# First norm from row sums, and a new order of the opening 80 microseconds, in a two-layer streaming encoder on one core

## The chip, the cores and the metric
One core of a Trainium2 chip runs the whole program. The metric is the device time of one execution in microseconds (us), the median of several runs. Five engines work side by side and meet at semaphores: TensorE (PE in the profile, its weight loads are PEld), VectorE (DVE), ScalarE (ACT), GpSimd (POOL) and SyncE (SP), which here only issues transfers. ScalarE issues transfers as well; SPq and ACTq are the rows of their queues.

## The reference
The input x is 512 frames of 1024 channels in float32, with one conditioning vector c. Each of two layers does the following; `ada` gives shift, scale and gate vectors from c.

```python
c_act = silu(c)
for l in range(DEPTH):                                   # DEPTH = 2
    ada = (c_act @ w_ada[l] + b_ada[l]).reshape(B, 9, 1024)
    u = modulate(rmsnorm(x, norm_g[l, 0]), ada[:, 0], ada[:, 1])   # xn * (1 + scale) + shift
    x = x + 0.5 * ada[:, 2] * swiglu(u, w_ff1_up[l], w_ff1_down[l])  # 1024 -> 2 x 2816 -> 1024
    u = modulate(rmsnorm(x, norm_g[l, 1]), ada[:, 3], ada[:, 4])
    x = x + ada[:, 5] * token_mixing(u, ..., sinks[l], cos, sin)   # windowed attention with rope, pooling, gates
    u = modulate(rmsnorm(x, norm_g[l, 2]), ada[:, 6], ada[:, 7])
    x = x + 0.5 * ada[:, 8] * swiglu(u, w_ff2_up[l], w_ff2_down[l])
```

cos and sin come from the integer positions and are first used in token mixing, as are the sinks (one logit a head).

## The kernel before
The activations lie transposed: a tile `x_t` holds 128 channels on the partitions and 512 frames along the free dimension, eight such pieces k = 0 to 7. A matrix product is a row of *tiles*: tile n gives 128 output channels for all 512 frames in one of five PSUM banks. Every product is made of float32 numbers split in a high and a low part, so that a tile has three matmuls a piece k: high weights by `u_hi`, high weights by `u_lo`, low weights by `u_hi`, 24 in all for 1024 input channels. ScalarE makes the high part of a weight tile, `w_hi` (L639, in the opening L781 in `first_weights`), and counts `hi_ready`; GpSimd makes the low part `w_lo` (L588) in place of the loaded weights and counts `lo_ready`. Weights arrive two tiles to a load in three slots `stage` (L491), ordered by SP: a slot is loaded again when TensorE has finished the tile that used it last.

The first half layer (`ff_half(0, 0, 0)`) has 22 up tiles (gate and value in turn) and 8 down tiles. For each pair ScalarE makes `silu` (L678), VectorE the product, `h_hi` and `h_lo` (L1003, L1006, L1008). Between these VectorE adds up 24 pieces of `w_ada` for the later vectors (`ada_piece`, L973 and L977, from the tile 3 of the half on), each loaded by SP in the same queue as the weights and each waiting until VectorE has used an older one.

The opening is written by hand, because the first norm and the first modulation vectors (`ada[:, 0]` and `ada[:, 1]`) are not there yet:
- `turn_x(j)` (L1601) transposes 128 frames of x_rows into two banks; VectorE copies one (L1263) and ScalarE the other (L761) to `x_t`. ScalarE squares `x_t` (L768), VectorE adds the squares over the eight pieces (`sum_squares`, L1222), and TensorE adds them over the partitions with a column of ones (L1671).
- Two calls of 12 small VectorE steps each (`rsqrt_step`, L826 to L837, two columns a call) give the reciprocal root, and TensorE spreads it over the partitions into ps6 (L1677).
- The modulation vectors come in four blocks b of 256 channels. For each block TensorE multiplies c_act by 2 MB of `ada_block` (`block_sums`, L1615, 64 small matmuls), VectorE copies the rows (L1231), TensorE turns them (`block_turn`, L1624), and VectorE makes shift and scale (L1236, L1238) and `xs` for the two pieces k of the block (L1249). ScalarE rounds them to `u_hi` (L789), VectorE makes `u_lo` (L1253).
- `block_tiles(b)` (L1638 to L1653) multiplies the two pieces of block b into four tiles at once (banks 0 to 3), so that tiles 0 to 3 are all done when block 3 is. TensorE's order is: sums, turn and tiles of block 0; sums and turn of 1; then sums and turn of b + 1 before the tiles of b; last the tiles of 3. Then tile 4 begins the ordinary order.
- Before tile 4 can start, `ff_half` of ScalarE first waits for tile 0 to make its silu and only then makes the high part of tile 4; the low part of tile 4 is GpSimd's. In block 0 VectorE makes the low parts of tiles 0 to 2, GpSimd that of tile 3.
- ScalarE's queue issues the small loads: c, constants and row vectors at the start; positions (L769, 256 KB broadcast) and sinks (L774, four loads of 256 single floats each) behind its last square. VectorE makes the rope angle in eight steps (`angle_step`) behind blocks 1 and 2, ScalarE its sine and half-angle sine in block 2 (L796, L797), VectorE finishes both behind block 3 (L1280 to L1284).
- SP issues, in order: x in four loads, block 0, stage slots 0 and 1, blocks 1 and 2, slot 2 (tiles 4 and 5), block 3. Its first `ada_piece` waits for all four block sums.

Of the kernel before, what the change touches and what calls it, by code (L numbers as in the profile page):

```python
# [160 lines left out]
def trunk(nc, x, c, positions, w_ada, b_ada, norm_g, w_ff1_up, w_ff1_down, w_in, q_norm_g, k_norm_g,  # L161
          sinks, w_pool_grp, pool_scale, w_attn_o, w_pool_o, w_out, w_ff2_up, w_ff2_down, consts, out):
    ctx = ExitStack()
    with ctx:
# [40 lines left out]
        x_sq = [at(f"x_sq{i}", [P, KT, P], F32, o) for i, o in enumerate((r_h + 5 * KT * BLOCK_W * 4, r_a))]  # L205
# [35 lines left out]
        pos_i = at("pos_i", [P, S], I32, r_g + KB2)  # L241
        angle = at("angle", [P, S], F32, r_g + 2 * KB2)
        turns = at("turns", [P, S], F32, r_g + 3 * KB2)
# [107 lines left out]
        x_summed = sem("x_summed")  # L351
# [54 lines left out]
        def newton_before(call):  # L406
            return call * NEWTON
# [52 lines left out]
        def _(sp):  # L460
# [99 lines left out]
            ada_block_load(2)  # L560
            up_load(first_up, 0, 0, 2)
            ada_block_load(3)
# [20 lines left out]
        def _(pool):  # L583
# [27 lines left out]
            pool.wait_ge(lo_ready, AHEAD)  # L611
            for l in range(DEPTH):
                for half in range(2):
                    for n in range(FF_TILES):
                        low_part("ff", tiles_before(l, 0, half), n + AHEAD)
# [17 lines left out]
        def _(act):  # L633
# [34 lines left out]
            def ff_half(l, i, half):  # L668
                tiles, loads = tiles_before(l, i, half), loads_before(l, i, half)
                for n in range(FF_TILES):  # L670
                    if START_TILES <= tiles + n + AHEAD < DEPTH * TILES:
                        round_weights("ff", tiles, loads, n + AHEAD)
                    if n < 2 * HALF_FT and n % 2 == 0:
                        j = n // 2
                        act.wait_ge(tile_done, tiles + n + DONE)
                        if j >= 2:
                            act.wait_ge(product_ready, products_before(l, i, half) + j - 1)
                        nc.scalar.activation(silu[:, j % 2, :], bank[n % BANKS][:, :], ACT.Silu  # L678
                                             ).then_inc(silu_ready, 1)
                    if n >= 2 * HALF_FT and half == 1 and event(l, i) + 1 < 3 * DEPTH:  # L680
                        square_tile(event(l, i) + 1, n - 2 * HALF_FT)

# [59 lines left out]

            act.dma_start(c_rows[:, :], c.rearrange("b (r c) -> (b r) c", c=P)).then_inc(c_in, 16)
            act.dma_start(consts_s[:, :], consts).then_inc(c_in, 16)
# [14 lines left out]
            for j in range(JT):  # L759
                act.wait_ge(turned, 2 * j + 2)  # L760
                nc.scalar.activation(x_t[:, 4:KT, j * P:(j + 1) * P],  # L761
                                     bank[(2 * j + 1) % 4][:, :].rearrange("p (m f) -> p m f", f=P), ACT.Copy
                                     ).then_inc(x_kept_act, 1)
                act.wait_ge(x_kept, j + 1)
                act.wait_ge(x_kept_act, j + 1)
                if j >= 2:
                    act.wait_ge(x_summed, j - 1)
                nc.scalar.activation(x_sq[j % 2][:, :, :], x_t[:, :, j * P:(j + 1) * P], ACT.Square).then_inc(x_squared, 1)  # L768
            act.dma_start(pos_i[:, :], positions[0].partition_broadcast(P)).then_inc(late_in, 16)  # L769
            with nc.allow_non_contiguous_dma(reason="eight sinks"):  # L770
                for i in range(DEPTH):
                    for t in range(2):

                        act.dma_start(sink_all[t * CHUNK:(t + 1) * CHUNK, i, :],  # L774
                                      sinks[i].rearrange("(b t) -> t b", t=2)[t].partition_broadcast(CHUNK)
                                      ).then_inc(late_in, 16)
# [6 lines left out]
            for b in range(BLOCKS):  # L783
# [10 lines left out]
                if b == 2:  # L794
                    act.wait_ge(setup_step, DEPTH + 8)
                    nc.scalar.activation(sin_t[:, :], angle[:, :], ACT.Sin).then_inc(act_step, 1)  # L796
                    nc.scalar.activation(cos_t[:, :], angle[:, :], ACT.Sin, scale=0.5).then_inc(act_step, 1)  # L797
# [20 lines left out]
        def _(dve):  # L818
# [52 lines left out]
            def stats_step(l, i, h, step):  # L871

                if step == 0:
                    dve.wait_ge(norm_summed, 2 * event(l, i) + (h + 1 if l or i else 2))
# [118 lines left out]
            def ff_half(l, i, half):  # L993
                tiles = tiles_before(l, i, half)
                count = products_before(l, i, half)
                for n in range(FF_TILES):
# [22 lines left out]
                    if n == 18 and half == 0:  # L1019
                        make_gate(l, i, half)  # L1020
                    if 0 <= n - ADA_STEP < ff_pieces(l, i, half):
# [197 lines left out]
            def sum_squares(j):  # L1219

                dve.wait_ge(x_squared, j + 1)
                nc.vector.tensor_reduce(sq_sum[:, j * P:(j + 1) * P], x_sq[j % 2][:, :, :].rearrange("p m f -> p f m"), AX_X,  # L1222
                                        ALU.add).then_inc(x_summed, 1)

# [16 lines left out]
            def block_u(b):  # L1241

                dve.wait_ge(first_vec, 2 * b + 2)
                for k in (2 * b, 2 * b + 1):
                    if k == 0:
                        dve.wait_ge(rstd_spread, 2)
                    if k >= 4:
# [7 lines left out]

            for l in range(DEPTH):
# [4 lines left out]
            for j in range(JT):  # L1261
                dve.wait_ge(turned, 2 * j + 1)
                nc.vector.tensor_copy(x_t[:, 0:4, j * P:(j + 1) * P],  # L1263
                                      bank[2 * j % 4][:, :].rearrange("p (m f) -> p m f", f=P)).then_inc(x_kept, 1)
                if j:
                    sum_squares(j - 1)
            sum_squares(JT - 1)
            for h in range(2):
                stats(0, 0, h)
            for b in range(BLOCKS):  # L1270
                block_vectors(b)
                block_u(b)
                if b == 0:
                    for n in range(AHEAD):
                        low_part("ff", 0, n)
                if b in (1, 2):
                    for step in range(4 * (b - 1), 4 * b):
                        angle_step(step)
            dve.wait_ge(act_step, 3)
            nc.vector.tensor_scalar(sin_t[:, :], sin_t[:, :], consts_s[:, K_SIGN:K_SIGN + 1], None, ALU.mult  # L1280
                                    ).then_inc(setup_step, 1)
            nc.vector.tensor_tensor(cos_t[:, :], cos_t[:, :], cos_t[:, :], ALU.mult).then_inc(setup_step, 1)
            dve.wait_ge(setup_step, DEPTH + 10)
            nc.vector.tensor_scalar(cos_t[:, :], cos_t[:, :], -2.0, 1.0, ALU.mult, ALU.add).then_inc(setup_step, 1)  # L1284
# [31 lines left out]
        def _(pe):  # L1316
# [276 lines left out]
            def turn_x(j):  # L1593

                pe.wait_ge(x_in[j], 16)
                for h in range(2):
                    g = 2 * j + h
                    if g >= 4:
                        pe.wait_ge((x_kept, x_kept_act)[h], j - 1)
# [26 lines left out]
            def block_tiles(b):  # L1626


                pairs = (2 * b, 2 * b + 1)
                for k in pairs:  # L1630
                    pe.wait_ge(u_hi_ready, 2 * k + 2)
                    if b == 0:
                        pe.wait_ge(u_lo_ready, 2 * k + 2)
                    for n in range(START_TILES):
                        hi, lo = hi_tile(n, KT), stage_tile(w_lo, "ff", n)
                        if b == 0 and k == 0:
                            pe.wait_ge(hi_ready, n + 1)
                        mm(bank[n][:, :], hi[:, k, :], u_hi[:, k, :], start=(k == 0), stop=False)  # L1638
                        if b == 0:
                            mm(bank[n][:, :], hi[:, k, :], u_lo[:, k, :], start=False, stop=False)  # L1640
                        else:
                            mm(bank[n][:, :], lo[:, k, :], u_hi[:, k, :], start=False, stop=False)
                    if b:
                        pe.wait_ge(u_lo_ready, 2 * k + 2)
                        for n in range(START_TILES):
                            last = mm(bank[n][:, :], hi_tile(n, KT)[:, k, :], u_lo[:, k, :], start=False, stop=(k == KT - 1))
                            if k == KT - 1:
                                last.then_inc(tile_done, 1)
# [90 lines left out]
```

## Time and profile before

| what | us |
|---|---|
| median of 3 runs (lowest to highest) | 2077.24 (2074.61 to 2077.28) |
| profiled execution, its own time | 2076.52 |
| its span, first to last instruction | 2074.7 |
| TensorE busy | 2038.8 |
| VectorE, GpSimd, ScalarE busy | 953.7, 673.8, 553.7 |
| chain that ended last: TensorE, VectorE, transfers | 95%, 3%, 1% |
| mean granted TensorE clock | 0.997 |

The profile lists, for each instruction, when it started and how long it ran, and for an idle engine what ended its idle time. The span of the profiled execution is 1.8 us shorter than its own time; the rest lies around the program.

### The profile page before, as it was taken

The numbers are of one execution on the slowest core, as the hardware profiler recorded it, in microseconds if no ns is written. First come the engines' busy times: TensorE is split into PE (matmuls) and PEld (weight loads), VectorE is DVE, ScalarE is ACT, GpSimd is POOL, SyncE is SP. The second block draws the span as 40 slices with busy tenths as digits, with TensorE's granted clock in tenths as the row PEclk, the third lists the DMA queues.
The fourth block names the chain that finished last, engine by engine and source line by source line (L and its number), as shares of the span: only waits on it lengthen the run. The fifth ranks groups of instructions, "written<-read, shape, count | busy, mean of one in ns | idle before, by whom it ended". The sixth has DMA issues, their size and how long they took to land.

```text
span 2074.7 us, 24433 instructions
## 1 busy us (share of the span) xinstructions
PE 2038.8 (98%) x10117; PEld 1700.4 (82%) x10117; DVE 953.7 (46%) x1389; ACT 553.7 (27%) x808; POOL 673.8 (32%) x274
## 2 busy tenths in 40 slices
PE   5999999999999999999999999999999999999999
PEld 4788888897888987888898888889878888888888
DVE  5654255366546755211256533445555666221121
ACT  2222122233422422122232211223243233221220
POOL 0345435502000245443434542452100004543451
PEclk9999999999999999999999999999999999999999
DMA  9465366522224366333326654652221435332331
GB/s 274 132 203 183 112 182 199 132 72 69 73 68 130 91 204 188 118 98 109 126 70 177 203 157 125 200 184 66 72 82 61 120 124 142 100 104 82 101 106 67
DMA packets 329066, 264.78 MB, mean 128 GB/s; under 512 B 24878, under 2 KB 310910, under 8 KB 328958
## 3 DMA queue, kind: packets, MB, share of 16 engines
q1 hardware_dynamic: 327296, 262.70, 42.6%
q8 instruction: 80, 1.31, 0.3%
q10 hardware_dynamic: 1662, 0.54, 0.1%
q14 instruction: 28, 0.23, 0.0%
HBM read 261.11 MB, written 2.10 MB: 127 GB/s over the span
## 4 chain that ended last, share of the span: by engine, by line
PE 95%; DVE 3%; DMA 1%; issue 1%; ACT 0%; POOL 0%; ACTq 0%; DVEq 0%
PE bank L1328 27%; PE bank L1330 27%; PE bank L1329 27%; PE bank L1404 1%; PE bank L1408 1%; PE bank L1405 1%; PE bank L1355 1%; PE bank L1357 1%; PE bank L1356 1%; PE ps L1537 1%; PE ps L1519 1%; DMA stage<-in_w_out 1%; PE ps L1495 0%; PE bank L1638 0%; PE ps L1502 0%
## 5 line engine op out<-in xcount | busy, mean ns | idle before, releaser
L588 POOL TENSOR_TENSOR w_lo<-stage,w_hi 128x1024 fp32r<-128x1024 f32 (+1 forms) x237 | 647.3, 2751 | 1210.3 <-ACT w_hi L639 1171.1
L1328 PE MATMUL bank<-u_hi,w_hi 128*128 128x512 f32 x1768 | 698.7, 395 | 3.7 <-POOL w_lo L588 3.5
L1330 PE MATMUL bank<-u_hi,w_lo 128*128 128x512 f32 x1768 | 689.3, 390 | 0.0
L1329 PE MATMUL bank<-u_lo,w_hi 128*128 128x512 f32 x1768 | 688.7, 390 | 0.0
L639 ACT ACTIVATE w_hi<-stage 128x1024 fp32r<-128x1024 f32 (+2 forms) x336 | 349.5, 1074 | 585.6 <-DMA stage<-in_w_ff_up 334.5
L1328 PEld LDWEIGHTS bank<-u_hi,w_hi 128*128 128x128 f32 x1768 | 332.4, 188 | 78.7 <-issue 10.8
L1329 PEld LDWEIGHTS bank<-u_lo,w_hi 128*128 128x128 f32 x1768 | 332.5, 188 | 69.6 <-issue 2.4
L1330 PEld LDWEIGHTS bank<-u_hi,w_lo 128*128 128x128 f32 x1768 | 332.2, 188 | 70.0
L1003 DVE TENSOR_TENSOR prod<-silu,bank 128x512 f32<-128x512 f32 x88 | 60.5, 688 | 522.3 <-PE bank L1330 503.9
L1328 PE MATMUL bank<-h_hi,w_hi 128*128 128x512 f32 x744 | 290.2, 390 | 1.0 <-DVE h_lo L1008 1.0
L1330 PE MATMUL bank<-h_hi,w_lo 128*128 128x512 f32 x744 | 289.5, 389 | 0.0
L1329 PE MATMUL bank<-h_lo,w_hi 128*128 128x512 f32 x744 | 289.5, 389 | 0.0
L919 DVE SCALAR_TENSOR_TENSOR x_t<-bank,gate,x_t 128x512 f32<-128x512 f32 (+1 forms) x92 | 62.6, 680 | 332.5 <-PE bank L1330 301.7
L977 DVE SCALAR_TENSOR_TENSOR ada_acc<-ada_stage,c_act,ada_acc 128x1024 f32<-128x1024 f32 x112 | 205.3, 1833 | 5.4 <-DVE ada_acc L977 0.9
L1328 PEld LDWEIGHTS bank<-h_hi,w_hi 128*128 128x128 f32 x744 | 139.6, 188 | 31.4 <-DVE h_lo L1008 1.5
L1330 PEld LDWEIGHTS bank<-h_hi,w_lo 128*128 128x128 f32 x744 | 139.7, 188 | 29.0
L1329 PEld LDWEIGHTS bank<-h_lo,w_hi 128*128 128x128 f32 x744 | 139.7, 188 | 28.8
L678 ACT ACTIVATE silu<-bank 128x512 f32<-128x512 f32 x88 | 52.5, 596 | 404.2 <-PE bank L1330 389.9
L843 DVE TENSOR_TENSOR w_lo<-stage,w_hi 128x1024 fp32r<-128x1024 f32 (+1 forms) x103 | 108.5, 1057 | 101.6 <-ACT w_hi L639 101.3
L1008 DVE TENSOR_TENSOR h_lo<-prod,h_hi 128x512 fp32r<-128x512 f32 x88 | 112.6, 1280 | 3.0
L1006 DVE CAST h_hi<-prod 128x512 fp32r<-128x512 f32 x88 | 72.8, 827 | 3.0
L650 ACT ACTIVATE squares<-x_t 128x512 f32<-128x512 f32 (+1 forms) x45 | 24.2, 538 | 155.9 <-DVE sq_sum L938 122.7
(176 smaller groups left out, 1488.2 us busy)
## 6 DMA issues: line engine op xcount, KB each, us to landing
stage<-in_w_ff_up SPq DMA_DIRECT2D x176, 512.0 KB
ada_stage<-in_w_ada SPq DMA_DIRECT2D x128, 512.0 KB, 4.8
stage<-in_w_ff_down SPq DMA_DIRECT2D x32, 1408.0 KB
stage<-in_w_in SPq DMA_DIRECT2D x18, 1024.0 KB
ada_block<-in_w_ada SPq DMA_DIRECT2D x8, 1024.0 KB, 12.1
stage<-in_w_out SPq DMA_DIRECT2D x8, 1024.0 KB
stage<-in_w_in SPq DMA_DIRECT2D x16, 256.0 KB
stage<-in_w_in SPq DMA_DIRECT2D x8, 512.0 KB
```

The costliest lines, as they stand in the source:

```text
L588: nc.gpsimd.tensor_tensor(stage_tile(w_lo, kind, n), t, hi_tile(n, depth(kind, n)), ALU.subtract).then_inc(lo_ready, 1)
L639: nc.scalar.activation(hi_tile(n, depth(kind, n)), stage_tile(stage, kind, n), ACT.Copy).then_inc(hi_ready, 1)
L678: nc.scalar.activation(silu[:, j % 2, :], bank[n % BANKS][:, :], ACT.Silu).then_inc(silu_ready, 1)
L843: nc.vector.tensor_tensor(stage_tile(w_lo, kind, n), stage_tile(stage, kind, n), hi_tile(n, depth(kind, n)), ALU.subtract).then_inc(lo_rea ...
L919: nc.vector.scalar_tensor_tensor(x_t[:, m, frames], product[:, frames], gate[:, i, m:m + 1], x_t[:, m, frames], ALU.mult, ALU.add).then_in ...
L977: nc.vector.scalar_tensor_tensor(ada_acc[:, :], ada_stage[a % ADA_SLOTS][:, :], c_k, ada_acc[:, :], ALU.mult, ALU.add).then_inc(ada_used, 1)
L1003: nc.vector.tensor_tensor(prod[:, j % 2, :], silu[:, j % 2, :], bank[n % BANKS][:, :], ALU.mult).then_inc(product_ready, 1)
L1006: nc.vector.tensor_copy(h_hi[:, j, :], prod[:, j % 2, :]).then_inc(h_hi_ready, 1)
L1008: nc.vector.tensor_tensor(h_lo[:, j, :], prod[:, j % 2, :], h_hi[:, j, :], ALU.subtract).then_inc(h_lo_ready, 1)
L1328: mm(bank[n % BANKS][:, :], hi[:, k, :], rhs_hi(k), start=(k == 0), stop=False)
L1329: mm(bank[n % BANKS][:, :], hi[:, k, :], rhs_lo(k), start=False, stop=False)
L1330: last = mm(bank[n % BANKS][:, :], lo[:, k, :], rhs_hi(k), start=False, stop=(k == k_n - 1))
```

## The change
The squares are taken by ScalarE from `x_rows`, where a frame's 1024 channels lie along the free dimension, with the accumulator giving the sum of each frame (`x_ss`, 128 x 4). One call of 12 steps works on all four columns. `sum_squares`, the products with the column of ones, and the second call are gone. TensorE turns all four parts of x in a row; VectorE copies six of the eight banks, ScalarE two. Constants are loaded ahead of c. VectorE makes the low parts of tiles 0 to 3; GpSimd starts with tile 4. ScalarE makes the high part of tile 4 in block 2, between the `u_hi` of blocks 2 and 3. Block 3 is loaded before slot 2. `block_tiles` is put in another order: tiles 0 and 1 first in block 0, starting when the first `u_hi` is there; from block 1 on the next block's sums lie between its two pieces k, and the next block's turn inside the second. Positions and sinks are loaded by ScalarE at tile 2 of the first half, the eight angle steps lie at tiles 6 to 13 of VectorE's half, the sines at tile 15 of ScalarE's, the last three steps at tile 17 of VectorE's.

```diff
-        x_sq = [at(f"x_sq{i}", [P, KT, P], F32, o) for i, o in enumerate((r_h + 5 * KT * BLOCK_W * 4, r_a))]
+        x_sq = [at(f"x_sq{i}", [P, D], F32, o) for i, o in enumerate((r_h + 5 * KT * BLOCK_W * 4, r_a))]
...
+            ada_block_load(3)
             up_load(first_up, 0, 0, 2)
-            ada_block_load(3)
...
-            pool.wait_ge(lo_ready, AHEAD)
+            pool.wait_ge(lo_ready, START_TILES)
...
-                    for n in range(FF_TILES):
+                    for n in range(0 if l or half else START_TILES - AHEAD, FF_TILES):
                         low_part("ff", tiles_before(l, 0, half), n + AHEAD)
...
# ScalarE, ff_half
-                    if START_TILES <= tiles + n + AHEAD < DEPTH * TILES:
+                    if START_TILES < tiles + n + AHEAD < DEPTH * TILES:
                         round_weights("ff", tiles, loads, n + AHEAD)
...
+                    if l + i + half == 0 and n == 2:
+                        positions_load()
+                    if l + i + half == 0 and n == 15:
+                        act.wait_ge(setup_step, DEPTH + 8)
+                        nc.scalar.activation(sin_t[:, :], angle[:, :], ACT.Sin).then_inc(act_step, 1)
+                        nc.scalar.activation(cos_t[:, :], angle[:, :], ACT.Sin, scale=0.5).then_inc(act_step, 1)
...
+            def positions_load():
+                act.wait_ge(u_lo_ready, U_STEPS)
+                act.dma_start(pos_i[:, :], positions[0].partition_broadcast(P)).then_inc(late_in, 16)
... (the four loads of the sinks, as before)
# ScalarE, opening
+            act.dma_start(consts_s[:, :], consts).then_inc(c_in, 16)
             act.dma_start(c_rows[:, :], c.rearrange("b (r c) -> (b r) c", c=P)).then_inc(c_in, 16)
-            act.dma_start(consts_s[:, :], consts).then_inc(c_in, 16)
...
             for j in range(JT):
+                act.wait_ge(x_in[j], 16)
+                if j >= 2:
+                    act.wait_ge(x_squared, j - 1)
+                nc.scalar.activation(x_sq[j % 2][:, :], x_rows[:, j, :], ACT.Square, accum_out=x_ss[:, j:j + 1]
+                                     ).then_inc(x_squared, 1)
+            for j in (2, 3):
                 act.wait_ge(turned, 2 * j + 2)
                 nc.scalar.activation(x_t[:, 4:KT, j * P:(j + 1) * P],
                                      bank[(2 * j + 1) % 4][:, :].rearrange("p (m f) -> p m f", f=P), ACT.Copy
                                      ).then_inc(x_kept_act, 1)
-                act.wait_ge(x_kept, j + 1)
-                act.wait_ge(x_kept_act, j + 1)
-                if j >= 2:
-                    act.wait_ge(x_summed, j - 1)
-                nc.scalar.activation(x_sq[j % 2][:, :, :], x_t[:, :, j * P:(j + 1) * P], ACT.Square).then_inc(x_squared, 1)
...
                 if b == 2:
+                    first_weights(START_TILES)
...
# VectorE, ff_half
+                    if l + i + half == 0 and 6 <= n < 14:
+                        angle_step(n - 6)
+                    if l + i + half == 0 and n == 17:
+                        angles_done()
...
# VectorE, opening
+            for g in (0, 1, 2, 3, 4, 6):
+                j, h = divmod(g, 2)
+                dve.wait_ge(turned, g + 1)
+                nc.vector.tensor_copy(x_t[:, 4 * h:4 * h + 4, j * P:(j + 1) * P],
+                                      bank[g % 4][:, :].rearrange("p (m f) -> p m f", f=P)).then_inc(x_kept, 1)
+            dve.wait_ge(x_squared, JT)
+            for step in range(NEWTON):
+                rsqrt_step(0, x_ss[:, :], slice(0, JT), D, step)
...
-                    for n in range(AHEAD):
+                    for n in range(START_TILES):
                         low_part("ff", 0, n)
...
# TensorE, block_tiles
+                if b == 0:
+                    for n0 in range(0, START_TILES, 2):
+                        for k in range(2):
+                            for part, ready in ((u_hi, u_hi_ready), (u_lo, u_lo_ready)):
+                                if n0 == 0:
+                                    pe.wait_ge(ready, 2 * k + 2)
+                                for n in (n0, n0 + 1):
+                                    if k == 0 and part is u_hi:
+                                        pe.wait_ge(hi_ready, n + 1)
+                                    mm(bank[n][:, :], hi_tile(n, KT)[:, k, :], part[:, k, :], start=(k == 0 and part is u_hi),
+                                       stop=False)
+                        for n in (n0, n0 + 1):
+                            pe.wait_ge(lo_ready, n + 1)
+                            for k in range(2):
+                                mm(bank[n][:, :], stage_tile(w_lo, "ff", n)[:, k, :], u_hi[:, k, :], start=False, stop=False)
+                    return
+                for k in (2 * b, 2 * b + 1):
                     pe.wait_ge(u_hi_ready, 2 * k + 2)
                     for n in range(START_TILES):
+                        mm(bank[n][:, :], hi_tile(n, KT)[:, k, :], u_hi[:, k, :], start=False, stop=False)
+                        mm(bank[n][:, :], stage_tile(w_lo, "ff", n)[:, k, :], u_hi[:, k, :], start=False, stop=False)
+                    if k % 2 and b + 1 < BLOCKS:
+                        block_turn(b + 1)
+                    pe.wait_ge(u_lo_ready, 2 * k + 2)
                     for n in range(START_TILES):
+                        last = mm(bank[n][:, :], hi_tile(n, KT)[:, k, :], u_lo[:, k, :], start=False, stop=(k == KT - 1))
+                        if k == KT - 1:
+                            last.then_inc(tile_done, 1)
+                    if k % 2 == 0 and b + 1 < BLOCKS:
+                        block_sums(b + 1)
```

## Rows read from the trace of the kernel before

**Rows 1.** The page: span, busy line, tenths of 40 slices for TensorE and its clock
```profile
span 2074.7 us, 24433 instructions
PE 2038.8 (98%) x10117; PEld 1700.4 (82%) x10117; DVE 953.7 (46%) x1389; ACT 553.7 (27%) x808; POOL 673.8 (32%) x274
...
PE   5999999999999999999999999999999999999999
```
**Rows 2.** Waits of TensorE from 76.2 us on: total us, times, longest
```profile
PE bank L1328 <- POOL w_lo L588: 3.5, 1, 3.5
PE ps L1373 <- DVE sq_sum L938: 1.6, 2, 1.0
```
**Rows 3.** Timeline 0 to 40 us: start, length, engine, instruction, idle time before
```profile
6.83 0.27 PE L1657 MATMUL ps<-consts_s,c_rows 8*128 8x8 f32 x1 [6.83 <-DMA consts_s<-in_consts]
...
7.03 3.67 PE L1601 MATMUL bank<-consts_s,x_rows 128*128 128x128 f32 x16
...
12.39 1.06 ACT L768 ACTIVATE x_sq<-x_t 128x1024 f32<-128x1024 f32 x1 [2.76 <-DVE x_t L1263]
...
15.35 0.69 DVE L1263 COPY x_t<-bank 128x512 f32<-128x512 f32 x1
...
18.37 3.68 DVE L1222 TENSOR_REDUCE sq_sum<-x_sq 128x128 f32<-128x1024 f32 x2
...
23.15 0.16 DVE L826 TENSOR_SCALAR nw_v<-ps 128x2 f32<-128x2 f32 x1 [1.11 <-PE ps L1671]
...
25.39 0.15 DVE L826 TENSOR_SCALAR nw_v<-ps 128x2 f32<-128x2 f32 x1
...
25.62 1.19 PE L1677 MATMUL ps<-consts_s,nw_y 128*128 128x128 f32 x4 [2.51 <-DVE nw_v L826]
...
28.93 3.53 PE L1615 MATMUL ps<-ada_block,c_act 128*32 128x128 f32 x64
...
34.56 1.38 ACT L789 ACTIVATE u_hi<-xs,shift_b 128x512 fp32r<-128x512 f32 x2 [10.83 <-DVE xs L1249]
...
35.38 1.42 DVE L1253 SCALAR_TENSOR_TENSOR u_lo<-xs,shift_b,u_hi 128x512 fp32r<-128x512 f32 x2 [0.26 <-ACT u_hi L789]
...
36.23 0.77 PE L1638 MATMUL bank<-u_hi,w_hi 128*128 128x512 f32 x1 [3.02 <-ACT u_hi L789]
...
36.71 3.49 DVE L843 TENSOR_TENSOR w_lo<-stage,w_hi 128x1024 fp32r<-128x1024 f32 x3
```
**Rows 4.** By line and form, ScalarE: count, busy us, mean ns, idle before
```profile
L693 ACT ACTIVATION_READ_ACCUMULATOR probs<-ps,neg_max 128x1 f32 x64 | 13.0, 203 | 0.0
```
**Rows 5.** Timeline 43 to 77 us, blocks 1 to 3 and tile 4
```profile
43.39 1.95 PE L1615 MATMUL bank<-ada_block,c_act 128*32 128x128 f32 x64
...
45.76 0.33 PE L1624 MATMUL ps<-consts_s,block_rows 128*128 128x128 f32 x1 [0.41 <-DVE block_rows L1231]
...
47.43 1.38 ACT L789 ACTIVATE u_hi<-xs,shift_b 128x512 fp32r<-128x512 f32 x2 [9.60 <-DVE xs L1249]
...
71.60 1.07 PE L1646 MATMUL bank<-u_lo,w_hi 128*128 128x512 f32 x4
72.03 0.60 ACT L678 ACTIVATE silu<-bank 128x512 f32<-128x512 f32 x1 [7.55 <-PE bank L1646]
...
73.65 5.14 POOL L588 TENSOR_TENSOR w_lo<-stage,w_hi 128x1024 fp32r<-128x1024 f32 x2 [30.97 <-ACT w_hi L639]
...
76.15 0.47 PE L1328 MATMUL bank<-u_hi,w_hi 128*128 128x512 f32 x1 [3.48 <-POOL w_lo L588]
```
**Rows 6.** Windows: length, busy by engine (count), granted TensorE clock, DMA share, GB/s
```profile
48.00:51.70 3.70, 0.00 (x0) 0.00 (x0) 3.29 (x7) 0.81 (x2) 0.00 (x0) 1.00 0.67 208
...
52.60:56.00 3.40, 3.40 (x10) 2.62 (x9) 3.14 (x5) 1.39 (x2) 0.00 (x0) 0.51 0.00 0
76.20:79.90 3.70, 3.70 (x10) 2.91 (x11) 3.50 (x4) 1.94 (x2) 3.39 (x2) 0.55 0.30 72
79.90:85.00 5.10, 5.10 (x24) 4.24 (x23) 5.00 (x3) 0.67 (x2) 4.40 (x2) 0.99 0.00 0
```
**Rows 7.** Windows of the transfers, same columns
```profile
24.00:33.00 9.00, 5.99 (x73) 4.95 (x73) 3.39 (x21) 0.00 (x0) 0.00 (x0) 1.00 0.47 120
34.00:50.00 16.00, 11.32 (x153) 8.83 (x153) 9.71 (x15) 4.66 (x6) 2.40 (x1) 0.89 1.10 338
...
51.00:61.00 10.00, 9.29 (x89) 7.31 (x89) 6.18 (x12) 2.54 (x4) 0.00 (x0) 0.83 0.01 3
```
**Rows 8.** Queues from 24 to 33 us: packets, MB, share; the sinks' issue and landing
```profile
q1 hardware_dynamic: 1071, 1.08, 40.9%
q10 hardware_dynamic: 978, 0.00, 5.7%
...
L774 ACTq DMA_DIRECT2D sink_all<-in_sinks x4: 637/656/753, 18.9 to 21.0; - x4
...
DMA to landing us min/median/max: 7.0/9.8/13.4
```
**Rows 9.** Timeline of SP, ScalarE, GpSimd, VectorE: the load for tiles 8 and 9
```profile
85.27 1.08 SPq L491 DMA_DIRECT2D stage<-in_w_ff_up  x2
...
92.33 2.01 ACT L639 ACTIVATE w_hi<-stage 128x1024 fp32r<-128x1024 f32 x2 [8.25 <-DMA stage<-in_w_ff_up]
...
93.47 4.76 POOL L588 TENSOR_TENSOR w_lo<-stage,w_hi 128x1024 fp32r<-128x1024 f32 x2 [9.17 <-ACT w_hi L639]
...
99.86 0.69 DVE L1003 TENSOR_TENSOR prod<-silu,bank 128x512 f32<-128x512 f32 x1 [6.42 <-PE bank L1330]
```

## Prediction on record
> **What bounds the kernel.** I read the page first. TensorE is busy 2038.8 of 2074.7 us, and only the first of the 40 slices shows it half idle [rows 1]. Then the waits of TensorE from tile 4 on: the largest is the 3.5 us in front of tile 4 itself, the next 1.6 us in two pieces [rows 2]. So behind the opening the time is a fixed train of matmuls, and whatever the opening gives, the end gives, unless a new wait appears in the first half. The question is when tile 4 starts and whether the train stays whole after it. Before, it starts at 76.15 us [rows 5]. Right behind its wait, from 76.2 to 79.9, the granted clock is 0.55, that is mostly at the lower level of 1.2 GHz; from 79.9 on it is 0.99 [rows 6]. 24 matmuls take 5.46 us on the fast clock (5.10 us hold 22.4 of them at 0.2275 us each); 3.7 us at 0.55 lose 1.7 us. Tile 4's start is thus worth 77.85 us on the fast clock.
>
> **The path before**, on the timeline [rows 3]: constants land at 6.83, transposes of half of x, then VectorE's reductions of squares (two of them 3.68 us, the last ends at 22.05), sums over partitions, two calls of 12 small steps (the first from 23.15, the second from 25.39), spreading, and the first block sums at 28.93. TensorE's first product starts at 36.23.
>
> **The first norm.** The constants are issued first instead of second: worth 0 to 0.65 us (the issue of c takes 0.6), I take 0.4. TensorE starts at 6.4, and 33 transposes at 3.67/16 = 0.23 us run to 14.0, if the copies keep pace: 0.69 us for a bank on VectorE against 0.92 us for its four transposes, so they do. The bank that VectorE copies last is turned at 13.1 and copied at 13.8. ScalarE's squares are 1.06 us each [rows 3]; reading the accumulator adds 0.20, as it does behind the exponentials [rows 4]. Four of them from 6.9 end at 12.0, ahead of that copy, so they lie beside it. The 12 steps took 25.39 - 23.15 = 2.24 us plus a tail of 0.1 with two columns; two or four columns make no difference I can see, since fixed cost is nearly all of it. They end at 16.1; the copies of the row vectors add 0.5, the spreading of four columns 1.2 (the row has 1.19). Block sums 0 start at 17.8 instead of 28.93: **11.1 us earlier**. Block 0's transfer is not in the way: it is second in SP's queue, and at some 300 GB/s its 2 MB behind 2.4 MB lie in place at 15.
>
> **Block 0.** The same steps follow with the same lengths, so the first `u_hi` (35.24 before) is there at 24.1 and TensorE starts there, without the wait for `u_lo`. ScalarE must have made the high parts of tiles 0 and 1 by then; they need slot 0, which lands by 21.7 at the latest (before, ScalarE took it up then, straight behind its issues). VectorE's `u_lo` ends at 25.7 (36.80 - 11.1). Its four low parts at 3.49/3 = 1.16 us end at 30.3; the fourth was GpSimd's. TensorE needs one more tile's low matmuls behind that: 30.8 at the earliest. With all 24 matmuls on the slow clock (0.43 us) it would be 34.5. I take 31.8, slow for the first eight as before. It was 43.4: **11.6 us earlier**.
>
> **Blocks 1 to 3** (29.0 us before, from 43.46 to 72.45). Work: 72 matmuls at 0.228 are 16.4 us, three sums at 1.95 are 5.85, turns 1.0. The new waits: sums to turned rows and back, 0.35; from the end of the turn (46.10) to the first `u_hi` (48.12) 2.02 us [rows 5], bare in block 1. In blocks 2 and 3 only the four `u_lo` matmuls (0.91 us) cover it, which leaves 1.1 us each. Sum 27.9 us, so **the last tile of block 3 ends at 59.8**. The order of before has no bare wait in blocks 2 and 3, but it lost 3.7 us bare at 48 to 51.7 and 1.7 us of clock behind it (0.51 in 52.6 to 56) [rows 6]. Whether the 2.0 us wait in block 1 also costs the clock no row decides: the idle 48 to 51.7 and 72.7 to 76.15 did, gaps of 0.4 did not. 0 or 1.7 us; I take 0, nearer in shape to neither, since a turn lies in its middle.
>
> **Transfers.** From 34 to 50 us they run at 338 GB/s, from 24 to 33 at 120, and after 51 at 3: all of the opening's 14 MB lies there at 51 [rows 7]. In the slow stretch the sinks' queue moves 978 packets and no bytes to speak of, and the weight queue is down to 41% [rows 8]. I read the dip as the sinks'; 9 us at 120 in place of 338 are 5.8 us. Without it the last transfer ends at 45, and counting back 1 MB (3.2 us) for slot 2 and 2 MB (6.2 us) for each block, block 3 is there at 42, block 2 at 35.6, block 1 at 29.4. Needed: block 1 at 31.8, block 2 at 39.3, block 3 at 48.2, slot 2 at 47.5. All hold. With the dip as it was, block 1 at 35.2 costs 3.4 us, the others little.
>
> **Tile 4.** Its high part is made at 47.5, GpSimd's low part (2.4 us) is done by 51. Nothing stands before it at 59.8, and the clock stays up. What covered nothing before (silu 0, `w_hi`, `w_lo`, 3.7 us) now falls to tile 5, behind tile 4's 5.46 us: `w_hi` 1.04 and GpSimd 2.4 to 2.85 end some 4 us after tile 3.
>
> **Moved into the first half.** ScalarE's issues take 3.2 us behind the silu of tile 2; the next load, for tiles 6 and 7, lands at about the same time and is needed 5 us later. VectorE's 11 angle steps of 0.4 to 0.7 us lie in gaps of 2 to 6 us between products. The sinks' dip now falls on the load for tiles 8 and 9. Before, it was issued at 85.27, its high part made at 92.33, its low part done at 95.85, and tile 8 began at 99.8 [rows 9]: 3.9 us to spare. If the dip moves as it is, it lies 7 to 16 us after tile 4's start, this load is issued at 9, and 1.5 MB (with an `ada` piece) lose up to 4 us: a stall of 0 to 1, up to 3 if the piece ahead suffers too. I take 0.5. The Trainium skill, "DMA: Bandwidth & Descriptors", says in "Rules for kernel authors" that a non-contiguous last dimension is lowered to one descriptor an element, and in "Queues, rings and completion order" that each engine takes turns between queues packet by packet; the 978 packets agree. By that rule the cost goes along with the load wherever it stands, which speaks against this part of the change; it would give the second rival below.
>
> **Sum.** 77.85 - 59.8 = 18.05, less 0.5, is 17.5 us. Span 2074.7 - 17.5 = 2057.2; 1.8 us lie around it, and the profiled execution (2076.52) is 0.7 under the median: 2059.7 us.
>
> **Rivals.**
> (1) The start-up has more bare waits than I count: a clock loss of 1.7 us in block 1, 1 to 2.7 us in block 0, or the blocks' data late by 3.4. Price 3 to 6 us: about 2064. For it: four hand-overs between VectorE, ScalarE and TensorE are now bare. Against: each is priced above from a row. 0.15.
> (2) The sinks' packets stall the train at tile 8 (or 6) by 2 to 4 us, with up to 1.7 us of clock: about 2063. For it: the margin of 3.9 us equals the loss. Against: the queues are emptier there, and before, the dip needed 5 us to set in. 0.15.
> (3) Nothing gained: slot 2, now last, holds up ScalarE, which waits for it in its own order ahead of the `u_hi` of block 3. This decides from a landing at 53 on, and 15 us are lost only from 68 on; the rows have everything at 51. 0.03.
> (4) Slower: VectorE's first angle step waits for the sinks, and behind it in VectorE's order stand the `ada` pieces, behind these in SP's order the weights. VectorE gets there some 14 us after tile 4's start; the loads have 4 us to spare; to lose 22 us the sinks would have to land 40 us after it, that is 35 us after their issue. The row's worst is 13.4. 0.03.
>
> **Numbers.** The forecast's own case has 0.64: 2056 to 2062. With (1) and (2) the range is 2056 to 2067. 0.2% is 4.2 us, about what a measurement of this kernel can tell from no change. Faster by more 0.94, within it 0.03, slower 0.03.
>
> **What the next profile would show.** Block sums 0 at about 17.8; first product at 24; no TENSOR_REDUCE before it; tile 4 at 59.8 without a wait and with the clock at 1.00; the dip of the transfers at 67 to 76 in place of 24 to 33, with q10's packets; TensorE's waits from tile 4 on as before or with one for `w_lo` at tile 8. Wrong would be: block sums behind a transfer, ScalarE waiting for slot 2 in block 2, VectorE waiting for the positions.

## The result, and the profile after

The changed kernel takes 2061.73 us (median of 4 runs, 2060.99 to 2064.09) against 2077.26 before: ratio 0.9926, 95% interval 0.9914 to 0.9939, so 15.5 us faster. The forecast was 2059.7, with 2056 to 2067 around it. The profiled execution has a span of 2059.9 us, 14.8 less than [rows 1].

The opening of the changed kernel on the timeline (start, length, engine, instruction, idle time before), to be laid beside [rows 3, 5]:

```profile
5.25 0.27 PE L1670 MATMUL ps<-consts_s,c_rows 8*128 8x8 f32 x1 [5.25 <-DMA c_rows<-in_c]
5.45 6.33 PE L1609 MATMUL bank<-consts_s,x_rows 128*128 128x128 f32 x32
...
11.33 0.19 ACT L780 ACTIVATION_READ_ACCUMULATOR x_sq<-x_rows 128x1 f32 x1
11.39 0.69 DVE L1268 COPY x_t<-bank 128x512 f32<-128x512 f32 x1 [0.68 <-PE bank L1609]
...
12.00 0.16 DVE L835 TENSOR_SCALAR nw_v<-x_ss 128x4 f32<-128x4 f32 x1
...
14.78 2.05 PE L1682 MATMUL ps<-consts_s,nw_y 128*128 128x128 f32 x8 [2.81 <-DVE vec L1275]
16.76 2.38 PE L1623 MATMUL ps<-ada_block,c_act 128*32 128x128 f32 x64
...
22.02 0.73 PE L1646 MATMUL bank<-u_hi,w_hi 128*128 128x512 f32 x2 [2.12 <-ACT u_hi L799]
...
28.21 1.07 PE L1651 MATMUL bank<-u_hi,w_lo 128*128 128x512 f32 x4
30.05 1.96 PE L1623 MATMUL bank<-ada_block,c_act 128*32 128x128 f32 x64 [0.78 <-DMA ada_block<-in_w_ada]
...
34.87 0.79 PE L1656 MATMUL bank<-u_hi,w_hi 128*128 128x512 f32 x1 [2.12 <-ACT u_hi L799]
...
45.55 0.50 PE L1656 MATMUL bank<-u_hi,w_hi 128*128 128x512 f32 x1 [1.18 <-ACT u_hi L799]
...
55.13 0.50 PE L1656 MATMUL bank<-u_hi,w_hi 128*128 128x512 f32 x1 [1.58 <-ACT u_hi L799]
...
60.69 0.39 PE L1336 MATMUL bank<-u_hi,w_hi 128*128 128x512 f32 x1
```

The reader sees: VectorE's small steps at 12.0 instead of 23.15, block sums 0 at 16.76 instead of 28.93, and tile 4 (L1336) at 60.7 without a wait, where it had been 76.15 with one of 3.5.

But a wait of the same size stands further on. The waits of TensorE from 59 us on (total, times, longest), beside [rows 2], and the first matmul of tile 8:

```profile
PE bank L1336 <- POOL w_lo L588: 3.5, 1, 3.5
PE ps L1381 <- DVE sq_sum L947: 0.6, 1, 0.6
```
```profile
86.41 0.77 PE L1336 MATMUL bank<-u_hi,w_hi 128*128 128x512 f32 x1 [3.52 <-POOL w_lo L588]
```

Windows of the changed kernel (length, busy by engine, granted clock, DMA share, GB/s), beside [rows 6, 7]:

```profile
35.00:38.40 3.40, 3.40 (x9) 2.68 (x10) 1.33 (x2) 0.47 (x1) 0.00 (x0) 0.53 1.10 348
...
66.50:74.50 8.00, 8.00 (x36) 6.31 (x35) 4.85 (x6) 2.49 (x3) 4.75 (x2) 1.00 0.11 15
...
87.00:90.50 3.50, 3.50 (x12) 2.81 (x11) 3.50 (x3) 1.81 (x2) 2.44 (x2) 0.66 0.26 99
```

From block 1 on, two stretches at mostly 1.2 GHz are left: one behind the bare wait of block 1, one behind the wait at tile 8. (A third lies in front of them: from 14.8 to 16.8 us, under the spreading, the granted clock is 0.50.) And the slow stretch of the transfers is no longer in the opening (348 GB/s there) but at 66.5 to 74.5 us, at 15 GB/s instead of the 120 of [rows 7]. The queues in it (packets, MB, share of 16 engines), and SP's issues:

```profile
q1 hardware_dynamic: 235, 0.11, 5.5%
q10 hardware_dynamic: 910, 0.00, 5.3%
```
```profile
67.48 0.34 SPq L510 DMA_DIRECT2D ada_stage<-in_w_ada  x1
67.87 4.94 SPq L491 DMA_DIRECT2D stage<-in_w_ff_up  x2
```

910 of the sinks' packets pass, and from 68 to 74 us not one packet of the weight queue does. The issue of the load for tiles 8 and 9 alone takes 4.94 us where it took 1.08 [rows 9], and its data come behind the sinks. The `ada` piece ahead of it was issued in the usual 0.34 us and stands still as well: it lands at 77.9 us.

### The profile page after: what moved, and what is told of

The parts are those of the page before. It is cut to its first block, busy times and chain, and to the rows that moved or that the text cites. A ratio compares the mean times of both kernels' runs of the same rounds, so it can differ in the third digit from the quotient of the medians.

```text
span 2059.9 us, 24401 instructions
## 1 busy us (share of the span) xinstructions
PE 2033.6 (99%) x10109; PEld 1695.8 (82%) x10109; DVE 955.3 (46%) x1376; ACT 551.8 (27%) x810; POOL 675.2 (33%) x273
## 4 chain that ended last, share of the span: by engine, by line
PE 95%; DMA 2%; DVE 1%; SPq 1%; ACT 0%; issue 0%; POOL 0%; DVEq 0%; ACTq 0%
PE bank L1336 27%; PE bank L1338 27%; PE bank L1337 27%; PE bank L1412 1%; PE bank L1413 1%; PE bank L1416 1%; PE bank L1363 1%; PE bank L1364 1%; PE bank L1365 1%; DMA stage<-in_w_ff_up 1%; PE ps L1545 1%; PE ps L1527 1%; SPq L491 1%; DMA ada_block<-in_w_ada 1%; PE ps L1434 0%; PE ps L1503 0%
## 5 line engine op out<-in xcount | busy, mean ns | idle before, releaser
L1336 PE MATMUL bank<-u_hi,w_hi 128*128 128x512 f32 x1768 | 698.9, 395 | 3.8 <-POOL w_lo L588 3.5
L1336 PEld LDWEIGHTS bank<-u_hi,w_hi 128*128 128x128 f32 x1768 | 332.5, 188 | 78.7 <-issue 7.3
L1336 PE MATMUL bank<-h_hi,w_hi 128*128 128x512 f32 x744 | 290.1, 390 | 0.0
L1336 PEld LDWEIGHTS bank<-h_hi,w_hi 128*128 128x128 f32 x744 | 139.7, 188 | 30.1 <-issue 1.2
```

The lines of the kernel that those rows point to most:

```text
L1336: mm(bank[n % BANKS][:, :], hi[:, k, :], rhs_hi(k), start=(k == 0), stop=False)
```

## The experiments

**The sinks in one load.** Every partition gets all 16 floats in one piece, and VectorE takes its heads from them when it negates them.

```diff
-                with nc.allow_non_contiguous_dma(reason="eight sinks"):
-                    for i in range(DEPTH):
-                        for t in range(2):
-                            act.dma_start(sink_all[t * CHUNK:(t + 1) * CHUNK, i, :], ...).then_inc(late_in, 16)
+                act.dma_start(sink_raw[:, :], sinks.rearrange("l h -> (l h)").partition_broadcast(P)).then_inc(late_in, 16)
...
-                        nc.vector.tensor_scalar(neg_sink[:, :], sink_all[:, l, :], -1.0, None, ALU.mult).then_inc(sink_ready, 1)
+                        raw = sink_raw[:, :].rearrange("p (l b t) -> p l t b", l=DEPTH, t=2)
+                        for t in range(2):
+                            r = slice(t * CHUNK, (t + 1) * CHUNK)
+                            ins = nc.vector.tensor_scalar(neg_sink[r, :], raw[r, l, t, :], -1.0, None, ALU.mult)
+                        ins.then_inc(sink_ready, 1)
```

> Of the changed kernel, with the four loads of 256 single floats for the sinks replaced by one load of all 16 floats to every partition (128 pieces of 64 bytes), at the same place. Theory: the wait of 3.5 us at tile 8 and the 1.6 us of clock behind it come from the sinks' packets, which hold the weight queue at nearly 0 GB/s from 66.5 to 74.5 us. Then the wait is gone and the time is 2061.7 - 5.1 = 2056.6 us. Rival A: the load for tiles 8 and 9 is late because it stands behind an ada piece in SP's queue: wait stays, 2061.7. Rival B: the 256 KB of the positions are the cause: wait stays, 2061.7.

Measured: 2056.0 us (2054.67 to 2057.45), ratio to before 0.9899 (0.9885 to 0.9914). The wait at tile 8 is gone. The queues of this kernel in the same stretch, 66.5 to 74.5 us, and SP's issue of the same load:

```profile
q1 hardware_dynamic: 2526, 1.88, 85.4%
q10 hardware_dynamic: 29, 0.00, 0.2%
```
```profile
67.99 1.08 SPq L491 DMA_DIRECT2D stage<-in_w_ff_up  x2
```

ScalarE's high part of tile 8 on the timeline, first in the changed kernel, then in this one:

```profile
82.78 2.00 ACT L639 ACTIVATE w_hi<-stage 128x1024 fp32r<-128x1024 f32 x2 [12.24 <-DMA stage<-in_w_ff_up]
```
```profile
75.02 2.01 ACT L639 ACTIVATE w_hi<-stage 128x1024 fp32r<-128x1024 f32 x2 [4.49 <-DMA stage<-in_w_ff_up]
```

The load was issued at the same time (67.87, 67.99) behind the same ada piece, and landed 7.8 us earlier. Rival A falls, and so does B: the positions are still loaded at the same place.

**The same in the kernel before.**

> The kernel before, with the sinks in one load. Theory: the slow stretch of the transfers at 24 to 33 us (120 GB/s) goes to 300 or more, and all of the opening's transfers end at 45 instead of 51 us; the time stays at 2077 within 1 us, since nothing in the opening of this kernel waited for a transfer. Rival: the slow stretch has another cause and stays.

Measured: 2077.53 us, ratio 1.0001 (0.9992 to 1.001). The window of 24 to 33 us, beside the first line of [rows 7], and one in which the transfers of the kernel before had still been running:

```profile
24.00:33.00 9.00, 5.68 (x73) 4.58 (x73) 3.59 (x22) 0.00 (x0) 0.00 (x0) 0.62 1.10 355
...
45.00:51.00 6.00, 2.77 (x88) 2.12 (x77) 4.48 (x10) 1.38 (x2) 0.00 (x0) 1.00 0.04 11
```

355 GB/s instead of 120, all but 0.07 MB moved by 45, and no time gained: the dip was real, and it was hidden. The same load that costs nothing in one kernel costs 5 us in the other.

**The sinks back in the opening**, positions left in the half.

```diff
             for j in (2, 3):
                 ... (ScalarE's two copies of x)
+            with nc.allow_non_contiguous_dma(reason="eight sinks"):
+                ... (the four loads, taken out of positions_load)
```

> Of the changed kernel, with the sinks' four loads back in the opening, behind ScalarE's two copies, and the positions left at tile 2. Theory: the slow stretch of the transfers moves with the sinks to some 18 to 27 us, the second block of w_ada lands at 35 instead of 30 us, TensorE waits for it 6 us instead of 0.8, and the wait at tile 8 (3.5 + 1.6 of clock) goes: the two cancel, 2061 to 2063. Rival B (the positions' 256 KB make the wait at tile 8): both waits, 2067.

Measured: 2062.25 us (2060.82 to 2065.72; the profiled execution is the 2065.72), ratio 0.9929 (0.9912 to 0.9945). The sum was right and its place wrong. No wait for w_lo is left at tile 8, with the positions where they were. But the transfers it slows are not only block 1's: TensorE's waits in this kernel from 15 us on hold

```profile
PE bank L1646 <- ACT u_hi L799: 4.6, 1, 4.6
...
PE bank L1646 <- ACT w_hi L791: 2.6, 2, 2.5
```

against 2.1 and none in the changed kernel. ScalarE waits for slot 0 ahead of the first u_hi, and for slot 1 ahead of tile 2. The rate of all transfers from 19 to 28 us, in 40 equal slices, shows how hard the sinks' packets (the last load lands at 25.9) press here:

```profile
GB/s 19 21 16 7 21 5 3 5 3 5 3 3 0 0 0 0 0 0 0 0 0 1 7 19 110 148 230 273 305 337 346 344 350 346 405 282 280 296 296 305
```

**The high part of tile 4 late again**, in the changed kernel and in the one with one load of the sinks.

```diff
-                    if START_TILES < tiles + n + AHEAD < DEPTH * TILES:
+                    if START_TILES <= tiles + n + AHEAD < DEPTH * TILES:
                         round_weights("ff", tiles, loads, n + AHEAD)
...
-                if b == 2:
-                    first_weights(START_TILES)
```

> Of the changed kernel, with the high part of tile 4 made where it was before the change, behind the silu of tile 0. Tile 4 gets back its wait of 3.5 us and 1.7 us of slow clock. But the load for tiles 8 and 9 is ordered at the same time, so tile 8 then has 5.2 us more to come: its wait of 3.5 us and the slow clock behind it should go. Theory: nothing lost in sum, 2061.7 to 2062.5. Rival: the two waits are independent, 2061.7 + 5.2 = 2066.9.

> As late_w4, with the sinks in one load. No wait at tile 8 is there to be relieved, so the late high part of tile 4 costs its full 3.5 + 1.7 us against one_load: 2056.6 + 5.2 = 2061.8. Rival: it costs nothing here either (then the early high part is worth nothing, 2056.6).

Measured: 2060.54 us (2058.66 to 2061.49) and 2062.4 us (2058.76 to 2062.49). Beside the slow sinks, taking this part of the change back costs nothing (the changed kernel had 2061.73); beside the quick ones it costs 6.4 us against 2056.0, where 5.2 were expected. (One of the four runs beside the quick sinks took 2058.76, so the 6.4 is loose.) In the first, tile 4 waits 3.5 us and tile 8 no more. So in the change as it was made the early high part bought 3.5 us of waiting at tile 4 and paid it back four tiles later. The expectation gave one reason for this, that tile 8 is reached later; the traces show two. The load for tiles 8 and 9 is issued at almost the same time (67.59 against 67.87), but it also lands 2.9 us earlier (ScalarE takes it up at 79.92, in the changed kernel at 82.78); the sinks were issued 1.5 us earlier there.

**The first norm alone**, in the kernel before: squares from x_rows, one call of steps, the transposes in a row, the copies as in the change.

> The kernel before, with the first norm of the changed one alone (squares from x_rows with the accumulator, one call of 12 steps, all of x turned in a row, the same copies). Block sums 0 start 11 to 12 us earlier. Theory: behind that the blocks of w_ada bind, since the sinks' loads still stand in the opening: block 1 lands at about 35, block 2 at 41, so most of the lead is lost in waits for them, 4 to 6 us faster than before, 2072. Rival: the lead stays whole, 2065.

Measured: 2067.29 us (2065.38 to 2069.26), ratio 0.9955 (0.9941 to 0.997), 9.2 us faster: between theory and rival, and outside both. The profile shows the mechanism and a different share (waits of TensorE from 15 us on, three of them):

```profile
PE bank L1634 <- ACT w_hi L782: 5.1, 1, 5.1
...
PE bank L1634 <- DVE u_lo L1250: 3.0, 1, 3.0
...
PE ps L1611 <- DMA ada_block<-in_w_ada: 2.3, 1, 2.3
```

The 3.0 us stood there before the change too (3.02 in [rows 3]). 5.1 us go to slot 1, 2.3 to block 2, both behind the sinks' packets; block 1 is there when it is asked for, since the wait for slot 1 lies ahead of it. I had counted the blocks and left out slot 1, which is ahead of them in SP's queue. SP had issued all of slots 0 and 1 by 17.0 us, before the sinks' packets set in at 19 us, and yet the rate fell far below the 120 GB/s of [rows 7] (again 19 to 28 us in 40 slices):

```profile
5.16 11.86 SPq L491 DMA_DIRECT2D stage<-in_w_ff_up  x4
```
```profile
GB/s 289 262 260 186 66 50 53 64 98 119 85 50 46 55 44 48 37 41 32 46 30 32 14 23 9 9 3 5 5 5 9 12 14 62 146 305 346 353 344 355
```

This run and before_one_load also settle the constants: with c issued first TensorE starts at 6.68 and 6.72, as in [rows 3] (6.83); in the ten traces with the constants first it starts between 5.04 and 5.25.

**The old order of blocks 1 to 3.**

```diff
-                    if k % 2 and b + 1 < BLOCKS:
-                        block_turn(b + 1)
...
-                    if k % 2 == 0 and b + 1 < BLOCKS:
-                        block_sums(b + 1)
...
-            for b in range(1, BLOCKS):
+            for b in range(1, BLOCKS - 1):
+                block_sums(b + 1)
+                block_turn(b + 1)
                 block_tiles(b)
+            block_tiles(BLOCKS - 1)
```

> Of the changed kernel, with TensorE's old order for blocks 1 to 3 (sums and turn of block b + 1 ahead of the tiles of b). Block sums 2 then come at 32 us and wait for their block until 36; tiles 1 start at 38.4 in place of 34.9, but no wait for u_hi is left in blocks 2 and 3 (2.8 us in the changed kernel). Theory: the end of block 3 moves by -1 to +2 us, and the wait at tile 8 moves with it: 2061 to 2064. Rival: the new order is worth its 2.8 us of waits or more, 2059.

Measured: 2061.85 us (2060.99 to 2064.04), no difference from 2061.73 that these runs can tell. The waits change places: no wait for u_hi in blocks 2 and 3, but one of 3.3 us for the transfer of block 2:

```profile
PE ps L1623 <- DMA ada_block<-in_w_ada: 3.3, 1, 3.3
```

The new order of the blocks brings nothing measurable here; the theory holds, the rival falls.

**An earlier turn**, on top of the one load of the sinks.

```diff
                         mm(bank[n][:, :], stage_tile(w_lo, "ff", n)[:, k, :], u_hi[:, k, :], start=False, stop=False)
-                    if k % 2 and b + 1 < BLOCKS:
-                        block_turn(b + 1)
+                        if n == 1 and k % 2 and b + 1 < BLOCKS:
+                            block_turn(b + 1)
```

> As one_load, and in blocks 1 and 2 TensorE turns the next block's rows behind the second of the four tiles instead of behind the fourth. The rows are ready 1.8 us before they are turned, and the waits for the first u_hi of blocks 2 and 3 are 1.2 and 1.6 us: with 0.9 us more of cover they shrink to 0.3 and 0.7, so 1.8 us faster than one_load, about 2054.8. Rival: VectorE or ScalarE is late for another reason there (a gap of 0.5 us before xs in block 3 has no releaser): then 1 us or less.

Measured: 2054.49 us (2053.73 to 2054.68), ratio 0.9891 (0.9877 to 0.9906). The two waits, 1.18 and 1.58 us in the changed kernel, shrink to 0.26 and 0.65 (timeline of this kernel):

```profile
44.65 0.50 PE L1654 MATMUL bank<-u_hi,w_hi 128*128 128x512 f32 x1 [0.26 <-ACT u_hi L793]
...
53.28 0.50 PE L1654 MATMUL bank<-u_hi,w_hi 128*128 128x512 f32 x1 [0.65 <-ACT u_hi L793]
```

**The three once more, in the same rounds on one chip.**

> The changed kernel once more, on the same chip and in the same rounds as the next two, since the intervals of one_load and of the changed kernel touch: 2061.7, with the wait for w_lo at tile 8 in its trace.

> Sinks in one load, repeated beside the changed kernel: 4.5 to 6 us faster than it. If the difference is under 2 us, the wait at tile 8 was a matter of one profiled execution.

> Sinks in one load and the early turn, repeated: 1.5 to 2 us faster than one_load_again, 6.5 to 7.5 faster than changed_again.

Measured: 2062.36 (2060.57 to 2062.97), 2057.52 (2057.0 to 2058.87) and 2054.64 us (2053.56 to 2054.95); the ranges do not touch. One load of the sinks is worth 4.8 us (5.7 in the first runs, which were not taken side by side), the early turn 2.9 more (1.5 in its first rounds). The 2.9 lies above the 1.5 to 2 expected; the trace of one_load_again has 2.0 us of waits for h_lo far behind the opening that the trace of early_turn_again has not, so not all of it need be the turn. The wait at tile 8 is 2.7 us in this execution of the changed kernel. The last kernel, at 0.9895 of before (0.9881 to 0.9908), beats both kernels of the case: 21.6 us faster than before.

## Why the prediction held, and where it did not

**The path bound by TensorE.** Right. What the opening gave, the end gave: tile 4 starts 15.5 us earlier.

**The constants.** Under-priced: 0.4 us taken, 0 to 0.65 as bounds, 1.4 to 1.8 measured (6.68 to 6.83 against 5.04 to 5.25). I had bounded it by the length of the issue in front; the landing moved by more, and no run shows why.

**The first norm.** 11.1 us forecast, 28.93 - 16.76 = 12.2 measured. The transposes run closer together (6.33 us for 32, I had 7.3), the accumulator costs 0.19 as the exponentials' did, squares lie beside the copies. One term was wrong: the spreading takes 2.05 us, not 1.2. The row I used counted one of the two old calls (4 matmuls); there is one call now and it has the matmuls of both (8). They run at a granted clock of 0.50 here; where the clock was 1.00 (late_w4) the same 8 took 1.13 us, so the 1.2 would have been right only on the fast clock.

**Block 0.** Ends at 29.3 against 31.8, since block sums 0 took 2.38 us instead of the 3.53 I had carried over and TensorE starts on the first u_hi at 22.0. The clock of this stretch differs from execution to execution: the spreading and sums take 2.05 and 2.38 us here, 1.13 and 1.95 in late_w4, 1.13 and 3.42 in early_turn.

**Blocks 1 to 3.** 27.9 us forecast, 60.7 - 30.05 = 30.6 measured. 1.6 of the difference are the clock behind the bare wait in block 1 (0.53 over 3.4 us), which I had left at 0 between bounds of 0 and 1.7; it was the upper one. In late_w4 the clock stayed up behind a longer wait, 3.5 us at tile 4 (granted 1.00 from 62.8 to 66.3 us), where the kernel before lost it [rows 6]: the same gap costs it in one execution and not in another. 0.5 more is the wait in block 3, 1.58 for 1.1: VectorE begins xs 0.5 us late there, in late_w4, early_turn and old_order as well, and no row shows why; this stays open. The last 0.6 us are in none of these terms.

**Transfers.** The dip is the sinks' (before_one_load), and the arrivals were good to 1 us: block 1 at 29.4 forecast, 30.05 measured, with a wait of 0.8. TensorE waited for no other transfer in the opening.

**Tile 4.** Right: no wait, clock at its upper level, 0.9 us later than forecast.

**Moved into the first half.** The step that was mis-sized: "1.5 MB (with an `ada` piece) lose up to 4 us: a stall of 0 to 1, up to 3 if the piece ahead suffers too. I take 0.5." It is about the load for tiles 8 and 9. Measured: 3.5 us of wait and 1.5 us of clock behind it (granted 0.64 over the 4.1 us from 86.4 to 90.5): 5.0 together, and 4.8 to 5.7 by the runs with one load. The reasoning carried the 120 GB/s of the opening over; at the new place the transfers ran at 15.

It is tempting to put this down to the state of the weight queue, full of issued transfers at the old place and empty at the new one. The runs speak against it. In norm_alone slots 0 and 1 were issued in full before the sinks' packets set in, and the rate went down to between 3 and 12 GB/s from 25 to 26 us; in sinks_opening SP was issuing without a pause and the rate went to 0 for about 2 us. So 120 GB/s was no property of a full queue, and which condition decides between 120 and nearly nothing is open.

The rule of the Trainium skill cited in the prediction ("DMA: Bandwidth & Descriptors", "Queues, rings and completion order") is that each engine takes turns between the queues packet by packet. The kernel before agrees with it to the packet: from 26 to 32 us its weight queue moved 559 packets and the sinks' queue 558. That the cost goes along with the load, as the prediction drew from it, came true as well: 910 packets in 8 us here, 978 in 9 us before. But turns would have let some 900 weight packets through here too, and 235 came, none of them between 68 and 74 us. So something other than the turns held the weights back. SP's issue of 4.94 us speaks for the issuing side; the `ada` piece, issued in 0.34 us and standing still all the same, speaks neither way. The cause stays open.

**Rivals.** (2) is what happened at tile 8, at 5.0 us (3.5 of wait, 1.5 of clock) where its price was 2 to 4 with up to 1.7 of clock. It had a chance of 0.15. (1) came true in its first part, 1.6 us of clock in block 1. (3): slot 2 was needed at 46.1 and there. (4): VectorE's first angle step waited 0.45 us for the sinks. Neither (3) nor (4) decided anything.

**The sum.** 15.5 + 1.7 (the clock behind tile 4 before) - 5.0 = 12.2 us, and the span fell by 14.8. The other 2.6 us lie behind the first half: TensorE's small waits there sum to 4.1 us before ([rows 2] has the largest) and 1.9 after. Most of them differ from trace to trace (waits of 0.9 to 2.1 us for h_lo in five of the ten with the new opening, the changed kernel run again among them, none in the other five), so they are not put down to the change. One does not: the waits for sq_sum are 1.6 and 1.5 us in the two traces with the old first norm and 0.6 in all eleven with the new one, so about 1 us may belong to the change, by a way that no run shows. The rest of the 2.6 is open.

**How much of this was luck.** The time, 2061.73 us, is 2 us from the forecast and even inside the narrower 2056 to 2062 of the forecast's own case. The mechanism, an opening that binds and a train that stays whole behind it, held for the opening; the train did not stay whole. The closeness of the number owes something to errors that cancelled: block 0 ended 2.5 us earlier than forecast, and from there to tile 4 it took 3.4 us longer; tile 8 cost 4.5 us more than its term, and 2.6 us that no term had came back later.

## What to carry to other kernels

A small transfer is not cheap by its bytes. Count its pieces: 1024 single floats in four loads held up the weights for 8 to 9 us, 128 pieces of 64 bytes in one load did not. (No run separates the number of pieces from the number of loads; the packets that pass during the stretch speak for the pieces.) Before such a load is moved, do not carry the rate of the old place over: count the time in which its packets pass as time in which the others may get nothing, and hold it against the next load's margin at the new place.

When a wait at the head of a paced train is removed, a load behind it that something else paces keeps its time of issue (67.59 and 67.87 us here) and loses the cover of the wait. Price the removal against the smallest margin downstream: here 3.5 us won at tile 4 came back at tile 8 until the sinks were cured, and two parts of the change that looked like gains (the early high part, the new order) measured as nothing beside the slow sinks. With the quick sinks the early high part was worth 6.4 us; the new order was not tried there.

## What the runs showed that I had not expected

The same 1024 packets left the transfers 120 GB/s at one place and 15 at another, and in two runs with the sinks in the opening close to nothing for 1 to 2 us, though weights were on order all the time. And TensorE, which waits for c (4 KB) and the constants (162 KB), could start 1.4 to 1.8 us earlier when the constants were issued first, 0.65 us earlier than before, on all traces read: 6.7 to 6.8 us with c first, 5.0 to 5.25 with the constants first.
